# A hybrid attention and experts layer on one core: decay columns, level steps, start and end rearranged

## The chip, the core and the metric

The kernel runs on one core of a Trainium2 chip. Its metric is the device time of one execution in microseconds, median of several runs. The engines are named as the profile names them: PE (TensorE; PEld are its weight loads), DVE (VectorE), ACT (ScalarE), POOL (GpSimd) and SP (SyncE, which here only issues DMAs). Each engine works through its own queue in order, and the queues wait for one another through semaphores.

## The reference, cut to what matters

256 tokens of width 2048 in float32 go through one layer. An RMS norm and one wide projection give the inputs of two attention-like mixers and of two gates. Mixer A (gated delta rule, 8 heads) needs, per chunk of tokens, the inverse of a unit lower triangular matrix that holds the decayed products of the keys. The mixers are projected, gated, merged, projected again and added to x. Then 32 experts, of which each token takes two, and a final RMS norm.

```python
h = _rmsnorm(x, norm_mix); z = h @ w_in
a_strict = where(strict, einsum("bhnid,bhnjd->bhnij", kb, k) * decay, 0.0)
t_mat = triangular_solve(eye + a_strict, eye, lower=True)
...
x = x + (sigmoid(mix_a) * ya + sigmoid(mix_b) * yb) @ w_out
x = x + _hier_moe(_rmsnorm(x, norm_ffn), ...)
return _rmsnorm(x, norm_final)
```

## The kernel before, in words

All work is written out by hand, queue by queue; nothing is planned by a compiler.

*Projection.* The weights come in chunks of 1 MB (four rows of 512 columns per partition) through a ring of four slots. A chunk is split in two parts that add up to the float32 value: ACT rounds it (`high`, line 671), DVE subtracts (`low`, line 942), and PE takes three products for each pair of operands (lines 1377 to 1379). So a chunk is 24 matmuls of 512 columns. ACT may be three chunks ahead of PE (NSPLIT). Four chunks make a block of 512 output columns, which ACT evacuates (lines 686 and 689). The token side is split likewise: PE transposes x (line 1400), ACT makes hT_hi (line 708), DVE makes hT_lo (line 956), in eight steps of two pieces.

*Order of the steps.* PE's attention steps (STEPS) are spread between the chunks: SPANS says how many chunks follow each step, and `fill` puts them there. Steps write two PSUM bank pairs in turn, so that a step waits until the one before the last is drained (`open_pair`). ACT and DVE follow the same order through `Splitter`: ahead of a result they split the chunks that PE will have used by then, except for the last, which `rest` makes up.

*Mixer A, per group g of four heads (eight units of 128 by 128).* PE transposes q, k and v (zqT, zkT, zvT, line 1540). POOL writes the decay of each token as 128 equal columns, gB (line 568), and PE multiplies gB with an upper triangle (gcb, line 1543), which gives the running sum of the decay in every row. DVE and ACT make the two decay matrices Dm and DT from it; DVE makes the convolution (line 1120), paced by the chunks behind gcb; ACT squares q and k (line 808), which ssq (line 1549) sums. Then ktok, vtok, khT, A (line 1559), PT (line 1560). DVE multiplies A with Dm (line 1139). The inverse is built in seven levels. For each, POOL masks Dm (line 605) into one of two buffers. Y1 (line 1562) is the first; each further level is Y (line 1567), a copy of it by ACT (line 813), dU (line 1570), dT (line 1573), two subtractions by DVE (lines 1154 and 1157) and one chunk of projection. Behind dU64 come wT (line 1589) and the rest of the step.

*Experts.* 16 pairs of experts. SP reads w1, w3 and w2, 24 pieces of 1 MB for a pair, into 16 slots. PE frees a slot when it has used it (`slotM_free`), and SP waits for that. PE multiplies with w1 and w3 (line 1753), transposes the hidden part, multiplies with w2 (line 1773: four steps t, each over all 2048 columns), and after ACT's copies (line 910) combines the result with the tokens' weights (line 1789), which DVE adds to x1 (line 1340). At the end ACT squares x1 (line 921), DVE sums (line 1350), POOL takes the root (lines 661 and 662), and DVE multiplies each row of 2048 by root and norm (line 1354), which SP stores (line 476).

## Time and profile before

| | us |
|---|---|
| median of 3 runs | 1897.27 |
| lowest, highest | 1896.11, 1897.51 |
| the profiled execution's own time | 1895.62 |
| its span | 1893.8 |

| engine | busy us | share |
|---|---|---|
| PE | 1785.6 | 94% |
| PE weight load | 1111.2 | 59% |
| DVE | 637.7 | 34% |
| ACT | 432.1 | 23% |
| POOL | 181.1 | 10% |

The granted clock of PE has a mean of 0.983 of full speed over the span. 537 MB are moved, at a mean of 284 GB/s. The shares are means over stages with different limits, so they don't tell what a change in one stage is worth. A line of the timeline has start, duration, engine, line of the kernel, operation, result and operands with their sizes, how many instructions are merged, and in brackets how long the engine had been idle before and what released it. Ends of matmuls are modelled. A float32 matmul stands as two records, so eight units of a step are 16 records, and eight transposes are 8.

### The profile page before, as it was taken

What the parts mean: (1) busy time and instruction counts of PE and PEld (TensorE: products, weight loads), DVE (VectorE), ACT (ScalarE), POOL (GpSimd) and SP (SyncE); (2) the same over time, 40 slices, a digit from 0 to 9 for tenths busy, and PEclk for the clock granted to TensorE, in tenths of its full rate; (3) what the DMA queues carried; (4) which work ended last, traced back from release to release, by engine and by line L of the source; (5) the groups of instructions that cost most, each with busy time, mean ns of one, the idle gap of its engine ahead of it and who ended that gap; (6) DMA issues with size and microseconds to landing.
All of it is one profiled execution on the core that took longest, in us unless ns stands there. A gap on an engine that the chain in (4) does not pass through costs nothing.

```text
span 1893.8 us, 21446 instructions
## 1 busy us (share of the span) xinstructions
PE 1785.6 (94%) x8774; PEld 1111.2 (59%) x8774; DVE 637.7 (34%) x670; ACT 432.1 (23%) x449; POOL 181.1 (10%) x235
## 2 busy tenths in 40 slices
PE   5999999989898899999899999999999999999996
PEld 4778877878787778888744344434344343443432
DVE  3256776533573355554302121112112021110112
ACT  4254354422442243334300000000000000000001
POOL 4000040430133010000000000000000000000000
PEclk8999999999999999999899999999999999999998
DMA  6445444422352245565999999999999999999996
GB/s 186 133 162 172 154 135 134 156 89 90 113 176 67 89 124 194 178 222 178 377 384 412 420 421 421 422 422 422 422 422 422 422 422 421 422 422 422 421 421 260
DMA packets 120460, 537.43 MB, mean 284 GB/s; under 512 B 8700, under 2 KB 8764, under 8 KB 70348
## 3 DMA queue, kind: packets, MB, share of 16 engines
q1 hardware_dynamic: 119808, 535.86, 72.5%
q0 software_dynamic: 592, 0.69, 0.3%
q8 instruction: 47, 0.77, 0.2%
q14 instruction: 13, 0.11, 0.0%
HBM read 534.42 MB, written 2.10 MB: 283 GB/s over the span
## 4 chain that ended last, share of the span: by engine, by line
PE 79%; DMA 15%; DVE 2%; ACT 2%; POOL 1%; issue 1%; DVEq 0%; SPq 0%; POOLq 0%; ACTq 0%
PE psum L1753 19%; DMA arena<-in_w 14%; PE psum L1377 12%; PE psum L1378 12%; PE psum L1379 12%; PE psum L1773 6%; PE psum L1789 6%; PE psum L1716 5%; PE psum L1570 1%; PE psum L1567 1%; PE psum L1573 1%; DMA arena<-in_w_in 1%; PE psum L1410 1%; PE psum L1469 1%; POOL arena L568 1%
## 5 line engine op out<-in xcount | busy, mean ns | idle before, releaser
L1753 PE MATMUL psum<-arena 128*64 128x512 f32 x2048 | 445.9, 594 | 13.3 <-DMA arena<-in_w 12.8
L942 DVE TENSOR_TENSOR w_lo<-arena,w_hi 128x2048 fp32r<-128x2048 f32 x120 | 276.1, 2303 | 326.7 <-ACT w_hi L671 320.3
L1377 PE MATMUL psum<-w_hi,hT_hi 128*128 128x512 f32 x832 | 336.6, 405 | 13.5 <-DVE hT_lo L956 12.2
L1378 PE MATMUL psum<-w_lo,hT_hi 128*128 128x512 f32 x832 | 332.0, 399 | 0.0
L1379 PE MATMUL psum<-w_hi,hT_lo 128*128 128x512 f32 x832 | 331.9, 399 | 0.0
L1753 PEld LDWEIGHTS psum<-arena 128*64 128x64 f32 x2048 | 143.9, 137 | 310.6 <-issue 282.2
L671 ACT ACTIVATE w_hi<-arena 128x2048 fp32r<-128x2048 f32 x120 | 229.4, 1915 | 292.0 <-PE psum L1379 286.3
L1773 PE MATMUL psum<-arena 128*64 128x512 f32 x1024 | 227.4, 598 | 13.0 <-DMA arena<-in_w 12.1
L1377 PEld LDWEIGHTS psum<-w_hi,hT_hi 128*128 128x128 f32 x832 | 158.7, 191 | 51.2 <-DVE hT_lo L956 12.3
L1379 PEld LDWEIGHTS psum<-w_hi,hT_lo 128*128 128x128 f32 x832 | 158.0, 190 | 38.6
L1378 PEld LDWEIGHTS psum<-w_lo,hT_hi 128*128 128x128 f32 x832 | 158.4, 190 | 36.4
L1773 PEld LDWEIGHTS psum<-arena 128*64 128x64 f32 x1024 | 71.3, 137 | 157.1 <-issue 128.1
L1324 DVE TENSOR_TENSOR arena<-psum,arena 128x512 f32<-128x512 f32 x64 | 44.2, 691 | 315.7 <-PE psum L1716 315.7
L1716 PEld LDWEIGHTS psum<-arena 128*128 128x128 f32 x1024 | 119.8, 194 | 26.1 <-issue 26.0
L1716 PE MATMUL psum<-arena 128*128 128x128 f32 x1024 | 127.3, 281 | 0.0
L1789 PE MATMUL psum<-arena 128*128 128x512 f32 x256 | 112.6, 593 | 0.0
L1340 DVE TENSOR_TENSOR arena<-arena,psum 128x512 f32<-128x512 f32 x128 | 87.9, 687 | 42.0 <-PE psum L1789 42.0
L900 ACT ACTIVATE arena<-psum 128x512 f32<-128x512 f32 x16 | 9.6, 597 | 358.9 <-PE psum L1753 358.9
L910 ACT ACTIVATE arena<-psum 128x512 f32<-128x512 f32 x64 | 38.2, 597 | 227.3 <-PE psum L1773 227.3
L641 POOL TENSOR_TENSOR arena<-arena 128x128 f32<-128x128 f32 x30 | 11.4, 399 | 783.4 <-PE psum L1716 751.0
L1331 DVE SCALAR_TENSOR_TENSOR arena<-arena,psum 128x512 f32<-128x512 f32 x16 | 11.0, 687 | 215.1 <-ACT arena L900 215.1
L1334 DVE TENSOR_TENSOR arena<-arena,psum 128x512 f32<-128x512 f32 x16 | 11.0, 687 | 214.2 <-PE psum L1753 214.2
(328 smaller groups left out, 1250.3 us busy)
## 6 DMA issues: line engine op xcount, KB each, us to landing
arena<-in_w SPq DMA_DIRECT2D x384, 1024.0 KB, 25.9
arena<-in_w_in SPq DMA_DIRECT2D x88, 1024.0 KB, 5.0
arena<-in_w_out SPq DMA_DIRECT2D x16, 1024.0 KB, 5.1
arena<-in_w_oa SPq DMA_DIRECT2D x8, 1024.0 KB, 5.0
arena<-in_w_ob SPq DMA_DIRECT2D x8, 1024.0 KB, 5.0
arena<-in_x SPq DMA_DIRECT2D x4, 1024.0 KB, 7.6
out_y<-arena SPq DMA_DIRECT2D x2, 1024.0 KB, 4.1
arena<-in_norm_final SPq DMA_DIRECT2D x1, 1024.0 KB, 18.6
```

What stands on the lines that cost most here:

```text
L671: nc.scalar.activation(w_hi[x % NSPLIT], ringA[:, x % RING_A, :], ACT.Copy).then_inc(sem("w_hi"), 1)
L910: nc.scalar.activation(Ysb[:, k * CB:(k + 1) * CB], bank(4 + k), ACT.Copy).then_inc(sem("yev"), 1)
L942: tt(w_lo[x % RING_A], ringA[:, x % RING_A, :], w_hi[x % NSPLIT].bitcast(F32), ALU.subtract)\
L1324: tt(xeT[u][:, 4 * b:4 * b + 4, :], bank(2 + b % 2).rearrange("p (k s) -> p k s", k=4), nffn[:, 4 * b:4 * b + 4].unsqueeze(2).to_broadcast ...
L1340: tt(x1[:, m, k * CB:(k + 1) * CB], x1[:, m, k * CB:(k + 1) * CB], bank(4 + (2 * k + m) % 4), ALU.add).then_inc(sem("xadd"), 1)
L1377: mm(m_banks[m], lhs[0][:, k0 + k, ms], wh[:, cs], start=(start and k == 0), stop=False)
L1378: mm(m_banks[m], lhs[0][:, k0 + k, ms], wl[:, cs], start=False, stop=False)
L1379: i = mm(m_banks[m], lhs[1][:, k0 + k, ms], wh[:, cs], start=False, stop=(stop and k == CT - 1))
L1716: i = mm(bank(2 + b % 2)[:, k * P:(k + 1) * P], h2[:, m, 4 * b + k, :], sel[:, m * P:(m + 1) * P], start=(m == 0), stop=(m == NM - 1))
L1753: i = mm(bank(w)[e * CAP:(e + 1) * CAP, :], xeT[u][:, CT * q + k, e * CAP:(e + 1) * CAP], src[e][:, k * CB:(k + 1) * CB], start=(q == 0 an ...
L1773: i = mm(bank(4 + k)[e * CAP:(e + 1) * CAP, :], aT[:, t * P + e * CAP:t * P + (e + 1) * CAP], src[e][:, k * CB:(k + 1) * CB], start=(t == ...
L1789: mm(bank(4 + j % 4), comb[u][:, m * P:(m + 1) * P], Ysb[:, k * CB:(k + 1) * CB], start=True, stop=True).then_inc(sem("cmb"), 1)
```

## The change

It touches five places.

1. *Start.* PE transposes the first half of x's tokens before it waits for the second half. ACT and DVE make three of the eight token steps ahead of chunk 0's split, two behind it, then split chunks 1 and 2, then make the last three; ACT's squares for the first norm come last. PE waits for hT_lo piece by piece. POOL builds its masks and the iota before it issues the DMAs of the twelve small tensors.
2. *Decay columns.* gB isn't written any more: the stationary operand of gcb is the decay column itself, read with a step of zero.
3. *First level.* POOL masks Dm for level 1 (mask[1]) right when Dm is scaled by beta, into gB; DVE multiplies A into gB first and into Dm second. POOL's mask loop begins at level 2. Each Y is copied in two halves, each as soon as PE has it, and dU waits for each half by itself.
4. *Chunks.* In group 1 gcb is followed by eight chunks instead of nine, dU64 by one instead of none.
5. *End.* The last pair's w2 is read in pieces of half the columns and two steps t (rows of 4 KB instead of 8), so that the first 1024 columns are complete after two of four pieces. Copies, combines and squares follow by quarters. The first 1024 columns are multiplied by the final norm ahead of the root, on POOL and DVE, and scaled by the root on ACT, the others are done on DVE as before; the output is stored in four halves. POOL takes one root for each half of the tokens, with 1/D and eps taken into the squares and the sum.

Some semaphores are merged, and SP's loop over the pairs ends one step earlier, with the last two pairs written out. The diff, cut to its core:

```diff
-     {"gcb": 9, "ssq": 1, "vtok": 1, "khT": 1, "PT": 0, "dT2": 1, "dT4": 1, "dT8": 1, "dT16": 1, "dT32": 1,
-      "wT": 1, "o": 2}.items()},
+     {"gcb": 8, "ssq": 1, "vtok": 1, "khT": 1, "PT": 0, "dT2": 1, "dT4": 1, "dT8": 1, "dT16": 1, "dT32": 1,
+      "dU64": 1, "wT": 1, "o": 2}.items()},
...
+            more_rounds = sp.value_load(rounds_i[0:1, 1:2], min_val=0, max_val=SEQ // CAP - 1)
+            end = more_rounds * (PAIRS // UNROLL) + (PAIRS // UNROLL - 1)
+            with sp.Fori(1, end) as i:
...
+            load_pair(PAIRS - 2, more_rounds * PAIRS + (PAIRS - 2), 0, 0, PER_PAIR)
+            load_pair(PAIRS - 1, more_rounds * PAIRS + (PAIRS - 2), 1, 0, 2 * RING_M - PER_PAIR + 8)
+            for j in range(16, PER_PAIR):
+                piece, e = divmod(j - 16, 2)
+                slot = (PER_PAIR + j) % RING_M
+                sp.wait_ge(sem("slotM_free"), more_rounds * (PAIRS * PER_PAIR) + ((PAIRS - 1) * PER_PAIR + j + 1))
+                sp.dma_start(ringM[slot].rearrange("p (t n) -> p t n", t=2),
+                             w2_h[2 * (PAIRS - 1) + e, :, 2 * (piece % 2):2 * (piece % 2) + 2,
+                                  (piece // 2) * HALF:(piece // 2 + 1) * HALF]).then_inc(sem(f"slotM{slot // 2}"), 16)
...
             for m in range(NM):
-                wait(sp, ("y_ready", m + 1))
-                sp.dma_start(y_v[:, m, :], x1[:, m, :]).then_inc(sem("y_out"), 16)
-            sp.wait_ge(sem("y_out"), 16 * NM)
+                for h, name in enumerate(("y_lo", "y_hi")):
+                    wait(sp, (name, m + 1))
+                    sp.dma_start(y_v[:, m, h * HALF:(h + 1) * HALF], x1[:, m, h * HALF:(h + 1) * HALF])\
+                        .then_inc(sem("y_out"), 16)
+            sp.wait_ge(sem("y_out"), 32 * NM)
...
+                           allow_small_or_imprecise_dtypes=True).then_inc(sem("pool_setup"), 1)
+            def small(dst, src, name):
+                pool.dma_start(dst, src, allow_slow_non_contiguous=True).then_inc(sem(name), 16)
...
-                for h in range(GH):
-                    for n in range(NM):
-                        u = h * NM + n
-                        i = nc.gpsimd.tensor_scalar(T_["gB"][:, u * P:(u + 1) * P], ones,
-                                                    mh(gdec)[:, n, g * GH + h:g * GH + h + 1], None, ALU.mult)
-                i.then_inc(sem("gB"), 1)
-
                 wait(pool, ("expD", g + 1))
...
                 bv = mh(beta)[:, :, g * GH:(g + 1) * GH].rearrange("p n h -> p h n").unsqueeze(3)\
                     .to_broadcast([P, GH, NM, P])
                 nc.gpsimd.tensor_tensor(T_["Dm"].rearrange("p (h n t) -> p h n t", h=GH, n=NM),
                                         T_["Dm"].rearrange("p (h n t) -> p h n t", h=GH, n=NM), bv,
                                         ALU.mult).then_inc(sem("DA"), 1)
+                pool.wait_ge(sem("DA"), g + 1)
+                nc.gpsimd.tensor_tensor(units(T_["gB"]), units(T_["Dm"]),
+                                        mask[1].unsqueeze(1).to_broadcast([P, GU, P]), ALU.mult)\
+                    .then_inc(sem("D1"), 1)
...
-                wait(pool, full(f"gcb.{g}"))
-                for i, b in enumerate(LEVELS):
+                for i, b in list(enumerate(LEVELS))[1:]:
...
-            wait(pool, ("ss4", 1))
-            link(nc.gpsimd.tensor_scalar(ss2, ss2, 1.0 / D, EPS, ALU.mult, ALU.add))
-            nc.gpsimd.tensor_tensor(rstd2, ss2, pw[:, 0:NM], ALU.pow).then_inc(sem("rstd3"), 1)
+            more_rounds = pool.value_load(rounds_i[0:1, 1:2], min_val=0, max_val=SEQ // CAP - 1)
+            more_rounds = pool.value_load(rounds_i[0:1, 1:2], min_val=0, max_val=SEQ // CAP - 1)
+            pool.wait_ge(sem("nfin_in"), 16)
+            for m in range(NM):
+                pool.wait_ge(sem("xadd"), more_rounds * (8 * PAIRS) + (8 * PAIRS + m + 1))
+                nc.gpsimd.tensor_tensor(xn[:, m, 0:CB], x1[:, m, 0:CB], nfin[:, 0:CB], ALU.mult)\
+                    .then_inc(sem("pool_end"), 1)
+            for m in range(NM):
+                pool.wait_ge(sem("dve_end"), NM + m + 1)
+                nc.gpsimd.tensor_tensor(rstd2[:, m:m + 1], ss2[:, m:m + 1], pw[:, 0:1], ALU.pow)\
+                    .then_inc(sem("pool_end"), 1)
...
+            def high_tokens(i):
                 act.wait_ge(sem("xTp"), i + 1)
                 for k in range(2):
                     j = nc.scalar.activation(hTh[:, 2 * i + k, :], bank(i)[:, k * SEQ:(k + 1) * SEQ], ACT.Copy,
                                              scale=nmix[:, 2 * i + k:2 * i + k + 1])
                 j.then_inc(sem("hTh"), 1)
+            act.wait_ge(sem("nmix_in"), 16)
+            for i in range(3):
+                high_tokens(i)
+            sp_ = Splitter(high, evac)
+            for i in range(3, 5):
+                high_tokens(i)
             sp_.second()
+            for i in range(5, 8):
+                high_tokens(i)
+            for m in range(NM):
+                nc.scalar.activation(Z1[:, m * D:(m + 1) * D], xs0[:, m, :], ACT.Square,
+                                     accum_out=ss1[:, m:m + 1]).then_inc(sem("ss1"), 1)
...
-                    result(f"Y{b}" + s)
-                    nc.scalar.activation(T_["Y"], pair(f"Y{b}" + s), ACT.Copy).then_inc(sem("Y"), 1)
+                    sp_.before(f"Y{b}" + s)
+                    act.wait_ge(sem("Y_half"), g * 6 + i + 1)
+                    nc.scalar.activation(T_["Y"][:, 0:512], pair(f"Y{b}" + s)[:, 0:512], ACT.Copy)\
+                        .then_inc(sem("Y"), 1)
+                    wait(act, full(f"Y{b}" + s))
+                    nc.scalar.activation(T_["Y"][:, 512:1024], pair(f"Y{b}" + s)[:, 512:1024], ACT.Copy)\
+                        .then_inc(sem("Y"), 1)
...
+            def squares(k, m):
+                act.wait_ge(sem("xadd"), last * 8 + (8 + 2 * k + m + 1))
+                nc.scalar.activation(junk[:, (2 * k + m) * CB:(2 * k + m + 1) * CB], x1[:, m, k * CB:(k + 1) * CB],
+                                     ACT.Square, scale=float(D) ** -0.5,
+                                     accum_out=ssq4[:, m, k:k + 1]).then_inc(sem("ss3"), 1)
+            def evict(k):
+                if k % 2 == 0:
+                    act.wait_ge(sem("down"), last * (NC - 1) + k // 2 + 1)
+                else:
+                    act.wait_ge(sem("slotM_free"), last * PER_PAIR + (RING_M + 16 + 4 * (k // 2 + 1)))
+                nc.scalar.activation(Ysb[:, k * CB:(k + 1) * CB], bank(4 + k), ACT.Copy).then_inc(sem("yev"), 1)
...
+                    squares(k, m)
+            act.wait_ge(sem("pool_end"), NM)
+            act.wait_ge(sem("dve_end"), NM)
+            for m in range(NM):
+                act.wait_ge(sem("pool_end"), NM + m + 1)
+                nc.scalar.activation(x1[:, m, 0:HALF], xn[:, m], ACT.Copy, scale=rstd2[:, m:m + 1])\
+                    .then_inc(sem("y_lo"), 1)
...
+                dve.wait_ge(sem("D1"), g + 1)
+                tt(T_["gB"], pair("A" + s), T_["gB"], ALU.mult).then_inc(sem("L_first"), 1)
...
+                dve.wait_ge(sem("L_first"), g + 1)
...
+                    if k == 2 and not more:
+                        dve.wait_ge(sem("nfin_in"), 16)
+                        for m in range(NM):
+                            dve.wait_ge(sem("xadd"), n * 8 + (8 + NM + m + 1))
+                            tt(xn[:, m, CB:HALF], x1[:, m, CB:HALF], nfin[:, CB:HALF], ALU.mult)\
+                                .then_inc(sem("dve_end"), 1)
...
-            dve.wait_ge(sem("ss3"), NM * NC)
-            nc.vector.reduce_sum(ss2, ssp.rearrange("p (m c) -> p m c", m=NM), axis=AX.X).then_inc(sem("ss4"), 1)
-            dve.wait_ge(sem("nfin_in"), 16)
-            wait(dve, ("rstd3", 1))
             for m in range(NM):
-                stt(x1[:, m, :], x1[:, m, :], rstd2[:, m:m + 1], nfin, ALU.mult, ALU.mult).then_inc(sem("y_ready"), 1)
+                dve.wait_ge(sem("ss3"), NM * NC - 1 + m)
+                nc.vector.reduce_sum(ss2[:, m:m + 1], ssq4[:, m], axis=AX.X).then_inc(sem("dve_end"), 1)
+            for m in range(NM):
+                wait(dve, ("pool_end", NM + m + 1))
+                stt(x1[:, m, HALF:D], x1[:, m, HALF:D], rstd2[:, m:m + 1], nfin[:, HALF:D], ALU.mult, ALU.mult)\
+                    .then_inc(sem("y_hi"), 1)
...
-            for i in range(8):
-                for k in range(2):
-                    for m in range(NM):
+                for i in range(8):
+                    for k in range(2):
                         j = tr(bank(i)[:, (k * NM + m) * P:(k * NM + m + 1) * P], xs0[:, m, 2 * i + k::KT], ident)
-                j.then_inc(sem("xTp"), 1)
-            wait(pe, ("hTl", 8))
+                    if m == NM - 1:
+                        j.then_inc(sem("xTp"), 1)
             for x in range(FIRST_BLOCKS * BCH):
+                if x < BCH:
+                    wait(pe, ("hTl", 2 * x + 2))
...
-                wait(pe, ("gB", g + 1))
-                lvl("gcb", lambda o, u, sl: mm(o[:, sl], T_["gB"][:, sl], upT, start=True, stop=True))
+                lvl("gcb", lambda o, u, sl: mm(o[:, sl], mh(gdec)[:, u % NM, g * GH + u // NM:g * GH + u // NM + 1]
+                                               .to_broadcast([P, P]), upT, start=True, stop=True))
...
-                pe.wait_ge(sem("L"), 7 * g + 1)
+                pe.wait_ge(sem("L_first"), g + 1)
                 lvl("Y1", lambda o, u, sl: mm(o[:, sl], T_["gB"][:, sl], ident, start=True, stop=True))
                 for j, b in enumerate(LEVELS[1:]):
                     L = T_["gB"] if (j + 1) % 2 == 0 else T_["L1"]
-                    pe.wait_ge(sem("L"), 7 * g + j + 2)
+                    pe.wait_ge(sem("L"), 6 * g + j + 1)
                     pe.wait_ge(sem("U"), 7 * g + j + 1)
-                    lvl(f"Y{b}", lambda o, u, sl: mm(o[:, sl], L[:, sl], T_["U"][:, sl], start=True, stop=True))
-                    pe.wait_ge(sem("Y"), 6 * g + j + 1)
+                    def level_y(o, u, sl):
+                        i = mm(o[:, sl], L[:, sl], T_["U"][:, sl], start=True, stop=True)
+                        if u == GU // 2 - 1:
+                            i.then_inc(sem("Y_half"), 1)
+                        return i
+                    def level_du(o, u, sl):
+                        if u % (GU // 2) == 0:
+                            pe.wait_ge(sem("Y"), 2 * (6 * g + j) + u // (GU // 2) + 1)
+                        return mm(o[:, sl], T_["T"][:, sl], T_["Y"][:, sl], start=True, stop=True)
+                    lvl(f"Y{b}", level_y)
                     pe.wait_ge(sem("T"), 6 * g + j + 1)
-                    lvl(f"dU{b}", lambda o, u, sl: mm(o[:, sl], T_["T"][:, sl], T_["Y"][:, sl], start=True,
-                                                      stop=True))
+                    lvl(f"dU{b}", level_du)
...
+            def last_down(n, u, arrived):
+                def combine(k):
+                    pe.wait_ge(sem("yev"), n * NC + (k + 1))
+                    for m in range(NM):
+                        j = 2 * k + m
+                        if j >= 4:
+                            pe.wait_ge(sem("xadd"), n * 8 + (j + 5))
+                        mm(bank(j % 4), comb[u][:, m * P:(m + 1) * P], Ysb[:, k * CB:(k + 1) * CB], start=True,
+                           stop=True).then_inc(sem("cmb"), 1)
+                for piece in range(4):
+                    src = arrived(16 + 2 * piece)
+                    half, tp = divmod(piece, 2)
+                    for k in range(2):
+                        for t in range(2):
+                            for e in range(2):
+                                i = mm(bank(4 + 2 * half + k)[e * CAP:(e + 1) * CAP, :],
+                                       aT[:, (2 * tp + t) * P + e * CAP:(2 * tp + t) * P + (e + 1) * CAP],
+                                       src[e][:, t * HALF + k * CB:t * HALF + (k + 1) * CB],
+                                       start=(tp == 0 and t == 0), stop=(tp == 1 and t == 1))
+                        if tp == 1 and k == 0:
+                            i.then_inc(sem("down"), 1)
+                    i.then_inc(sem("slotM_free"), 2)
+                    if piece:
+                        combine(piece - 1)
+                combine(NC - 1)
...
```

## Rows read from the trace of the kernel before

**Rows 1.** busy by stage; columns: window, busy us (instructions) per engine, clock, DMA, GB/s
```profile
256.00:700.00 444.00, 404.55 (x2173) 343.90 (x2172) 231.09 (x210) 164.24 (x148) 114.90 (x78) 0.97 0.36 114
...
1290.00:1871.00 581.00, 554.46 (x2682) 231.06 (x2680) 88.75 (x129) 35.90 (x65) 21.33 (x56) 1.00 1.01 421
1871.00:1893.80 22.80, 10.72 (x32) 4.02 (x32) 10.26 (x11) 8.17 (x20) 0.91 (x2) 0.81 0.24 100
```

**Rows 2.** timeline of the start; columns: start, us, engine, line, operation [idle before, releaser]
```profile
2.43 2.54 POOL L500 DMA_DIRECT2D arena<-in_w_in  x2 [0.30 <-POOL arena L496]
...
10.02 5.98 PE L1400 MATMUL psum<-arena 128*128 128x128 f32 x32 [10.02 <-DMA arena<-in_x]
10.23 0.56 POOL L500 DMA_DIRECT2D arena<-in_b_re  x1
...
11.96 10.60 POOL L532 TENSOR_SCALAR_AFFINE_SELECT arena<-arena 128x128 f32<-128x128 f32 x14
17.60 1.91 ACT L671 ACTIVATE w_hi<-arena 128x2048 fp32r<-128x2048 f32 x1 [5.69 <-DMA arena<-in_w_in]
19.41 5.92 ACT L708 ACTIVATE hT_hi<-psum,arena 128x256 fp32r<-128x256 f32 x16
19.54 2.29 DVE L942 TENSOR_TENSOR w_lo<-arena,w_hi 128x2048 fp32r<-128x2048 f32 x1 [19.54 <-ACT w_hi L671]
21.75 6.35 DVE L956 SCALAR_TENSOR_TENSOR hT_lo<-psum,arena,hT_hi 128x256 fp32r<-128x256 f32 x16
...
28.16 0.80 PE L1377 MATMUL psum<-w_hi,hT_hi 128*128 128x512 f32 x1 [12.16 <-DVE hT_lo L956]
```

**Rows 3.** busy time of all engines in two stretches of the start
```profile
9.00:14.00 5.00, 3.98 (x19) 4.01 (x20) 0.00 (x0) 2.00 (x2) 4.92 (x13) 1.00 1.09 153
...
17.00:23.00 6.00, 0.00 (x0) 0.00 (x0) 3.46 (x5) 5.40 (x12) 5.83 (x9) 0.59 1.04 388
```

**Rows 4.** timeline, groups 0 and 1: the gcb matmuls, and the copy of zkT.1
```profile
287.70 3.68 PE L1543 MATMUL psum<-arena 128*128 128x128 f32 x16 [2.77 <-POOL arena L568]
...
498.20 3.78 PE L1543 MATMUL psum<-arena 128*128 128x128 f32 x16 [3.81 <-POOL arena L568]
...
493.53 1.22 DVE L1099 COPY arena<-psum 128x1024 f32<-128x1024 f32 x1
```

**Rows 5.** line 813, ScalarE's copy of Y: instructions, and who waited for them (us, times)
```profile
L813 ACT ACTIVATE arena<-psum x12: 1023/1023/1023, 386.6 to 653.8; 128x1024 f32<-128x1024 f32 x12
...
  PE psum L1570: 13.4, 12
```

**Rows 6.** GpSimd's masks (line 605) of 570 to 590 us; timeline of group 1's first levels
```profile
L605 POOL TENSOR_TENSOR arena<-arena x2: 2350/3336/4322, 580.7 to 585.0; 128x1024 f32<-128x1024 f32 x2
...
579.41 1.22 DVE L1139 TENSOR_TENSOR arena<-psum,arena 128x1024 f32<-128x1024 f32 x1 [2.25 <-PE psum L1559]
...
585.09 3.50 PE L1562 MATMUL psum<-arena 128*128 128x128 f32 x16 [3.93 <-POOL arena L605]
589.96 2.02 PE L1567 MATMUL psum<-arena 128*128 128x128 f32 x16 [1.36 <-issue]
```

**Rows 7.** timeline of PE behind the last level of group 1
```profile
660.12 2.07 PE L1589 MATMUL psum<-arena 128*128 128x128 f32 x8 [3.20 <-DVE arena L1154]
```

**Rows 8.** timeline of the end of the convolution and of the squares in group 1
```profile
541.87 1.92 ACT L671 ACTIVATE w_hi<-arena 128x2048 fp32r<-128x2048 f32 x1 [3.71 <-PE psum L1379]
...
546.75 2.00 ACT L808 ACTIVATE arena<-arena 128x1024 f32<-128x1024 f32 x2
...
552.86 3.63 PE L1549 MATMUL psum<-arena 128*128 128x1 f32 x32
```

**Rows 9.** chain that ended last (start, us, what); timeline of the two products
```profile
1871.09 3.65 PE psum L1773 x16
1874.74 7.08 PE psum L1789 x16
...
1884.68 4.61 DVE L1354 SCALAR_TENSOR_TENSOR arena<-arena 128x2048 f32<-128x2048 f32 x2 [1.20 <-POOL arena L662]
```

## What the change will do to the time: the prediction

> **What bounds the kernel now.** I read the busy time by stage first [rows 1]. From 256 to 700 us the tensor engine (PE) is busy 404.6 of 444.0 us while DMA uses 0.36 of its time: the attention stage is bound by PE, and what can be won there are its 39 us of gaps. From 1290 to 1871 us, in the experts, DMA is busy throughout (share 1.01, 421 GB/s) and PE is not (554 of 581 us): there the weights set the pace, and the change leaves their bytes alone. Behind the last weights stands a tail of 22.8 us at 100 GB/s. Next I went through the timeline of each place that the diff touches, for the wait that ends last there. The kernel is a chain: start, attention with gaps, weight stream, tail. The experts' weights are read into slots that PE's progress frees, so what is won before them starts the stream earlier by as much; I count such gains in full.
>
> The sum is made against the profiled execution: span 1893.8, its own time 1895.6 us, which is 1.65 us under the median of 1897.27.
>
> **The start.** In [rows 2] the first weight chunk is in at 17.60 us, ScalarE (ACT) rounds it (1.9) and VectorE (DVE) forms the rest (2.3, from 19.54): 21.8. PE starts only at 28.16, because DVE then forms all sixteen hT_lo pieces (6.35) behind ACT's sixteen hT_hi pieces (5.92). With three of the eight groups made ahead of the chunk, PE waits for chunk 0 alone: 28.16 − 21.8 = 6.4 us, if the chunk lands as before.
> It should land earlier, since POOL now issues the small tensors' DMAs behind its masks. In [rows 3] the traffic falls to 153 GB/s from 9 to 14 us with the DMA engines fully busy, and is back at 388 from 17 to 23. x is in at 10.0 [rows 2]. A chunk is 1.05 MB, 2.6 us at 400 GB/s: 12.5. By then the three groups are nearly ready: the transposes of x's first half run before its second half is in, the others take half of 5.98 us, and ACT's six pieces take 6 × 0.37 = 2.2 us from 10.4 on, to 12.7. Rounded at 14.6, rest at 16.9, PE starts at 17.0: gain 11.1 us. Bounds 6.4 (chunk as before) and 11.8.
> What must stay hidden: ACT makes tokens 3 and 4 (1.5), rounds chunks 1 and 2 (to about 22), makes tokens 5 to 7 (2.2) and both squares (as wide as a rounding, 2.1 each), to 28.3, and then waits for the small tensors. POOL's masks, which took from 10.8 to 22.6 [rows 2], now stand ahead of its issues, which took from 2.43 to 10.8: the last is out at 22.9. I let it land by 31, an estimate: 8 us, as long as chunk 0 took from x's landing on. Chunk 3 is then ready at 31 + 1.9 + 2.3 = 35.2, and PE asks for it at 17.0 + 7.3 + 2 × 5.6 = 35.5 (7.3: the first chunk begins at the 1.2 GHz level; 5.6: the period of ACT's rounding in [rows 8]). The cover is thin: each later us costs one.
> The Trainium skill speaks against this move (SBUF — State Buffer, SBUF: two separate sides): the descriptors of a DMA issued from GpSimd are written by that engine, and a VectorE operation in a two-port mode locks it out of the shared ports. VectorE had nothing to do before 19.54 [rows 2] and now works from 10.9 on; no row here shows such a delay. By the rule the result is the second rival.
>
> **Decay columns.** POOL no longer writes gB; PE loads the decay column with a step of zero. In [rows 4] PE waits 2.77 us for POOL at 287.70 and 3.81 at 498.20, and the 16 records then take 3.68 and 3.78 us, where the same shape takes 2.02 at 589.96 [rows 6]: the 1.2 GHz level against 2.4. PE itself was free at 284.9 and 494.4; in group 1 DVE's copy of zkT ends at 494.8 and is now late. Group 0: 284.9 + 2.3 = 287.2 instead of 291.4, 4.2 us. Group 1: 494.8 + 2.1 = 496.9 instead of 502.0, 5.1. Sum 9.3 us. A load with step zero has no row; the nearest, loads of 128 columns, hide beside the matmuls. I take no extra. Bounds 7.5 (0.1 us more for each of 16 units) and 10.3.
>
> **Level copies in halves.** In [rows 5] PE waited 13.4 us for ACT's copy of Y, 12 times 1.11. The copy of the first half can start when four units are done, 1.1 us into Y's 2.0, and takes 0.6 (half of 1.02 and a little): over at 1.75, so that dU starts when Y ends. The second half is copied from 2.0 to 2.6, and dU wants it at 2.9. All but 0.05 of each gap goes: 12.7 us. Each period shrinks from 12.4 to 11.3; ACT's two halves, one rounding and now and then an evacuation fill 4.4 of it. Bounds 10 (where ACT is evacuating at the time) and 13.4.
>
> **First level masked ahead.** In [rows 6] PE waits 3.93 us for POOL's first mask in group 1 and runs Y1 at the lower level, 3.50 us. Now DVE multiplies A with the already masked decay (1.2 us from 579.41), and behind it comes the ordinary product, which also frees the bank: 581.8. Y1 then ends at 583.7. Next late is POOL's mask for level 2, which starts after the second product, beside DVE: [rows 6] have 4.32 us for the mask beside DVE and 2.35 for the one alone. Started at 581.8 it is done at 586.2 at most, and U, which DVE makes behind a low part and PT's product, at 586.4. Y2 starts there instead of at 589.96: 3.5 us. If the new wait of 2.7 us lowers the clock, Y2 costs 1.7 more; I take 2.5. Bounds 0 and 3.5. In group 0 a chunk covers this wait already: 0.
> The Trainium skill explains the two lengths (same page and section: VectorE and GpSimd lock a shared pair of ports for a whole instruction). If the lock never bit, the mask would be done at 584.1 and the sum would be the same, as U is later.
> POOL's added mask (2.4 to 4.3 us) delays rqk; DVE scales ktok up to 3 us later, and khT follows only behind a chunk of 5.6 us: 0, at most 1.
>
> **The moved chunk.** Behind dU64 of group 1 PE waits 3.20 us for DVE and then takes 2.07 us [rows 7] for eight records, half of a level's sixteen, which is again the lower level: 1.0 too much. A chunk there covers both, 4.2. But gcb keeps eight chunks to cover the convolution. PE reaches ssq at 552.86 in [rows 8]; a chunk less is 547.3, while ACT's squares end at 546.75 + 2.00 = 548.75. Exposed 1.3, net 2.9 us. Bounds 1 and 4.2.
>
> **The tail.** Before [rows 9]: last weights at 1871.09, matmuls 3.65, eight combines 7.08, then add, square, sum, power and two products to 1889.3, and 4.5 for the store. After: pieces of 2.1 MB come 4.98 us apart (421 GB/s), and PE needs 3.65 + 1.77 (a quarter of 7.08) for each, so it begins the last 0.9 late. With 3.65 and two combines' pairs (3.5) the last combine ends 8.0 after the last weights, before 10.7: 2.7 us. Behind it, before, 12.0 us. Now add, square, sum and power, 2.0 for the first row of tokens and 0.8 more for the second, and two products of half the width on each of two engines (2 × 1.2): the last store goes out at 4.3 and carries 0.5 MB, 3.7: 8.0, a gain of 4.0. The final norm's MB is last in the queue, 2.5 us behind the weights, and the columns multiplied ahead fit before the last combines. The last 8 MB have rows of 4 KB instead of 8; the nearest rates are 388 for the chunks' 2 KB rows [rows 3] and 421, a loss of 0 to 1.7 us; I take 0.5. Tail 6.2 us. Bounds 3 and 8.
>
> Merged semaphores and the restated loop on SP's queue move no wait: 0.
>
> **Sum.** 11.1 + 9.3 + 12.7 + 2.5 + 2.9 + 6.2 = 44.7 us: 1897.3 − 44.7 = 1852.6 us.
>
> **Rivals.**
> *Copies stay visible* (0.10). If the wait inside dU, or an ACT that is busy when half of Y is done, brings back what the halves win, 12.7 us stay: 1865.3. For it: ACT also evacuates blocks there. Against: in [rows 5] all 12 gaps are the bare copy, so ACT was never late.
> *The small tensors come late* (0.14). If they land at 36 us instead of 31, or chunk 0 lands as before, some 4.7 us of the start's gain go: 1857.3. For it: the thin cover.
> *Step zero is slow* (0.03), the one that ends slower than before: if the array reads a column of step zero slowly, 16 units pay. From 44.7 / 16 = 2.8 us each the whole gain is gone; at 4 us the change costs 64 − 44.7 = 19.3 us: 1916.6. Against: loads in [rows 4] show no price beside the matmuls.
> *The stream is not moved* (0.02): if the weights' stream kept its time, only the tail would count, 1891 to 1897. Against: its slots are freed by PE alone.
>
> **Numbers.** The forecast has 0.71. The range goes from 1844 (all upper bounds together are 51 us, 1846, and 2 for scatter) to 1868 (visible copies, and 2.7 of other lower bounds). 0.2%, 3.8 us, is about what a measurement of this kernel can tell from no change: faster 0.95, within it 0.02, slower 0.03.
>
> **What would show it.** First projection matmul at 17 us; gcb without a wait, at 2.1 to 2.3 us; none of PE's waits at dU; one wait of 2 to 3 us ahead of Y2 in group 1; 1.3 us ahead of ssq in group 1 and none behind dU64; the span's end 16 us behind the last weights. It is wrong if PE waits for w_lo of chunk 3, or if the experts begin less than 35 us earlier.

## The result, and the profile after

The changed kernel takes 1856.2 us where the kernel before, on the same chip, takes 1897.4: a ratio of 0.9779, 95% interval 0.9762 to 0.9796 (four executions of each; those of the changed kernel lie between 1852.4 and 1856.8). A second set, taken later beside the last experiments, gave 1856.5 against 1896.9, 0.9788 (0.9774 to 0.9801). The forecast was 1852.6 with a range of 1844 to 1868, and "faster". The profiled execution of the changed kernel takes 1856.06 us with a span of 1854.2; before it was 1895.62 and 1893.8. So the traces differ by 39.6 us, and the sum of the prediction was 44.7.

The same three stages as in [rows 1], by the busy time in windows (window, busy us and instructions of PE, PEld, DVE, ACT and POOL, clock, DMA share, GB/s):

```profile
243.00:664.00 421.00, 404.46 (x2187) 344.87 (x2186) 232.96 (x212) 168.78 (x161) 101.31 (x62) 0.98 0.39 123
1254.00:1834.00 580.00, 555.01 (x2682) 231.59 (x2680) 90.09 (x131) 38.63 (x71) 21.32 (x56) 1.00 1.01 421
1834.00:1854.15 20.15, 10.43 (x36) 3.32 (x30) 9.14 (x12) 7.62 (x16) 5.54 (x4) 0.86 0.32 127
```

PE's work in the attention stage is the same 404.5 us, but it now takes 421 us and not 444: the gaps went. The experts run at the same 421 GB/s, only earlier.

The start, answering [rows 2] (start, us, engine, line, operation, idle before and its releaser):

```profile
9.56 1.28 ACT L716 ACT_TABLE_LOAD   x1 [9.56 <-PE psum L1474]
10.86 2.31 ACT L716 ACTIVATE hT_hi<-psum,arena 128x256 fp32r<-128x256 f32 x6
13.02 1.94 ACT L685 ACTIVATE w_hi<-arena 128x2048 fp32r<-128x2048 f32 x1
...
17.43 0.76 PE L1452 MATMUL psum<-w_hi,hT_hi 128*128 128x512 f32 x1 [6.37 <-DVE w_lo L998]
...
20.02 0.56 POOL L541 DMA_DIRECT2D arena<-in_b_re  x1
```

PE multiplies from 17.43 instead of 28.16. The chunk is in before ACT asks for it at 13.02 (no idle time ahead of w_hi). A load of ACT's table, 1.28 us, now stands between the transposed tokens and the first high half.

The decay columns and group 1, answering [rows 4], [rows 6], [rows 7] and [rows 8]; TensorE's timeline and GpSimd's mask:

```profile
274.99 1.98 PE L1618 MATMUL psum<-arena 128*128 128x128 f32 x16
474.77 2.05 PE L1618 MATMUL psum<-arena 128*128 128x128 f32 x16 [0.41 <-DVE arena L1162]
523.28 6.12 PE L1625 MATMUL psum<-arena 128*128 128x1 f32 x32 [1.50 <-ACT arena L828]
...
555.65 2.02 PE L1638 MATMUL psum<-arena 128*128 128x128 f32 x16 [0.75 <-DVE arena L1204]
560.07 2.02 PE L1645 MATMUL psum<-arena 128*128 128x128 f32 x16 [2.40 <-DVE arena L1212]
...
625.49 1.05 PE L1675 MATMUL psum<-arena 128*128 128x128 f32 x8
...
555.59 4.33 POOL L611 TENSOR_TENSOR arena<-arena 128x1024 f32<-128x1024 f32 x1 [11.00 <-DVE arena L1204]
```

The gcb products (L1618) have no wait for GpSimd and take 2 us instead of 3.7. Y1 (L1638) waits 0.75 and Y2 (L1645) 2.40, for VectorE's U and not for the mask beside it, which is over at 559.92, only 0.05 us before U (558.75 + 1.22 = 559.97). wT (L1675) has no wait. Ahead of ssq (L1625) there is one of 1.50 us, and ssq itself takes 6.12 us where it took 3.63 [rows 8]: that was in no part of the prediction.

The levels, answering [rows 5]: ACT's copy of a half (line 834) and who waited for it.

```profile
L834 ACT ACTIVATE arena<-psum x12: 597/599/599, 372.9 to 617.3; 128x512 f32<-128x512 f32 x12
...
  PE psum L1653: 0.5, 3
```

13.4 us in 12 waits have become 0.5 in 3 (0.15 us each).

The tail, answering [rows 9]; timelines of TensorE, VectorE, GpSimd and the stores on SP's queue:

```profile
1821.02 8.78 PE L1834 MATMUL psum<-arena 128*64 128x512 f32 x32 [0.88 <-ACT arena L927]
...
1837.15 3.65 PE L1834 MATMUL psum<-arena 128*64 128x512 f32 x16
1840.73 3.70 PE L1825 MATMUL psum<-arena 128*128 128x512 f32 x8
...
1845.33 0.58 POOL L675 TENSOR_TENSOR arena<-arena 128x1 f32<-128x1 f32 x1 [3.98 <-DVE arena L1425]
1846.02 1.28 DVE L1428 SCALAR_TENSOR_TENSOR arena<-arena 128x1024 f32<-128x1024 f32 x1
1846.19 1.53 POOL L675 TENSOR_TENSOR arena<-arena 128x1 f32<-128x1 f32 x1 [0.28 <-DVE arena L1425]
...
1847.20 2.94 SPq L493 DMA_DIRECT2D out_y<-arena  x4
```

The traffic behind the stores' issue (window, busy us of the five engines, clock, DMA share, GB/s):

```profile
1848.00:1853.00 5.00, 0.00 (x0) 0.00 (x0) 1.04 (x1) 0.91 (x1) 0.00 (x0) 0.56 1.00 400
```

The four pieces (L1834) no longer wait for a DMA, where the last one did in [rows 9]: PE is late, not the weights. Its first two pieces take 8.78 us and the last 3.65.

**Where the 39.6 us came from.** Take the same matmul in both traces and subtract its start: the lead of the changed kernel. It is 10.7 us at the first projection matmul, 10.1 at zkT of group 0 (the low clock level lasted 1.3 us longer at the earlier start, and the first chunk took 7.96 us instead of 7.35), 14.4 behind gcb, 12.8 at A, 20.0 behind the levels of group 0, 25.2 behind gcb of group 1, 26.3 at A, 29.9 at Y2, 36.9 at the last dU, 34.6 at wT, 36.2 at u0, 36.3 when w3 is through, and 39.6 at the end. Twice it falls or stands still where the change does nothing good: between gcb and A of group 0 (−1.6) and of group 1 (+1.1, though a chunk of 5.6 us less stands there).

### The profile page after: what moved, and what is told of

It reads as the page before. It is cut to its first block, busy times and chain, and to the rows that moved or that the text cites. A ratio compares the mean times of both kernels' runs of the same rounds, so it can differ in the third digit from the quotient of the medians.

```text
span 1854.2 us, 21397 instructions
## 1 busy us (share of the span) xinstructions
PE 1782.7 (96%) x8774; PEld 1109.0 (60%) x8774; DVE 640.2 (35%) x676; ACT 436.2 (24%) x463; POOL 170.2 (9%) x221
## 4 chain that ended last, share of the span: by engine, by line
PE 81%; DMA 13%; DVE 2%; ACT 2%; SPq 1%; issue 1%; POOL 0%; POOLq 0%; DVEq 0%; ACTq 0%
PE psum L1868 18%; DMA arena<-in_w 13%; PE psum L1452 12%; PE psum L1453 12%; PE psum L1454 12%; PE psum L1890 7%; PE psum L1905 5%; PE psum L1802 5%; PE psum L1653 1%; PE psum L1659 1%; PE psum L1645 1%; PE psum L1834 1%; SPq L459 1%; DVE w_lo L998 1%; PE psum L1486 1%
## 5 line engine op out<-in xcount | busy, mean ns | idle before, releaser
L1868 PE MATMUL psum<-arena 128*64 128x512 f32 x2048 | 446.1, 594 | 13.3 <-DMA arena<-in_w 12.8
L1868 PEld LDWEIGHTS psum<-arena 128*64 128x64 f32 x2048 | 143.9, 137 | 310.7 <-issue 282.3
L1890 PE MATMUL psum<-arena 128*64 128x512 f32 x960 | 211.3, 595 | 10.5 <-DMA arena<-in_w 10.5
L1890 PEld LDWEIGHTS psum<-arena 128*64 128x64 f32 x960 | 66.0, 137 | 144.5 <-issue 118.9
L1905 PE MATMUL psum<-arena 128*128 128x512 f32 x240 | 105.5, 592 | 0.0
```

The costliest lines, as they stand in the source:

```text
L1868: i = mm(bank(w)[e * CAP:(e + 1) * CAP, :], xeT[u][:, CT * q + k, e * CAP:(e + 1) * CAP], src[e][:, k * CB:(k + 1) * CB], start=(q == 0 an ...
L1890: i = mm(bank(4 + k)[e * CAP:(e + 1) * CAP, :], aT[:, t * P + e * CAP:t * P + (e + 1) * CAP], src[e][:, k * CB:(k + 1) * CB], start=(t == ...
L1905: mm(bank(4 + j % 4), comb[u][:, m * P:(m + 1) * P], Ysb[:, k * CB:(k + 1) * CB], start=True, stop=True).then_inc(sem("cmb"), 1)
```

## The experiments

All edits are to the changed kernel. Each row gives the median, the ratio to the kernel before on the same chip in the same set, and the difference to the changed kernel. That difference goes by the time saved against before: 41.2 us for the first eight rows, 40.4 for the last four, which had the changed kernel beside them.

| kernel | us | ratio (95%) | against the changed one |
|---|---|---|---|
| small_first | 1861.0 | 0.9807 (0.9790 to 0.9825) | +5.3 |
| decay_pool | 1865.0 | 0.9834 (0.9816 to 0.9851) | +9.2 |
| whole_copy | 1872.3 | 0.9870 (0.9853 to 0.9888) | +16.6 |
| late_mask | 1858.8 | 0.9804 (0.9787 to 0.9822) | +3.0 |
| chunk_back | 1859.6 | 0.9795 (0.9779 to 0.9812) | +3.1 |
| chunk_from_khT | 1855.6 | 0.9773 (0.9757 to 0.9790) | −0.9 |
| wide_ssq | 1853.5 | 0.9771 (0.9755 to 0.9787) | −3.0 |
| tail_warm | 1856.6 | 0.9775 (0.9758 to 0.9793) | +0.1 |
| after_again | 1856.5 | 0.9788 (0.9774 to 0.9801) | 0 |
| chunk_ahead | 1853.0 | 0.9763 (0.9749 to 0.9776) | −3.5 |
| wide_ahead | 1849.2 | 0.9748 (0.9735 to 0.9761) | −7.3 |
| combined | 1845.7 | 0.9735 (0.9721 to 0.9748) | −10.8 |

The intervals of the ratios are 3.2 to 3.4 us wide to either side, 2.5 in the last four rows, and the executions of one kernel can lie 7 us apart (1851.35 to 1858.40 in tail_warm). So differences of 3 us (late_mask, chunk_back, wide_ssq, and chunk_ahead's 3.5) are not shown by the times alone; for those the traces are read.

**1. The start (small_first).** The block of twelve small loads goes back ahead of the masks:

```
+            def small(dst, src, name):
+                pool.dma_start(dst, src, allow_slow_non_contiguous=True).then_inc(sem(name), 16)
...
             def masks(upper):
...
-            def small(dst, src, name):
-                pool.dma_start(dst, src, allow_slow_non_contiguous=True).then_inc(sem(name), 16)
```

> Only one part of the changed kernel is undone: GpSimd issues the twelve small loads ahead of the masks again, as before. My theory: ahead of the token and weight loads they take the transfer queues' time at the start (the weights' first chunk came at 17.6 us before), so the first projection matmul moves from 17.4 us back to 21.5 to 22.5, ScalarE's table load and order being as in the changed kernel; the whole kernel is 4 to 5 us slower than the changed one (1860 to 1861.5). The rest of the 10.7 us gained at the start (some 6) is then the order of ScalarE's squares. Rival: the order of the small loads is of no account and all 10.7 came from the order on ScalarE: the first projection matmul stays at 17.4 and the time at 1856.

5.3 us slower. The start of its timeline:

```profile
18.56 1.91 ACT L685 ACTIVATE w_hi<-arena 128x2048 fp32r<-128x2048 f32 x1 [3.58 <-DMA arena<-in_w_in]
...
22.94 0.76 PE L1452 MATMUL psum<-w_hi,hT_hi 128*128 128x512 f32 x1 [8.66 <-DVE w_lo L998]
```

ACT waits for the chunk until 18.56 and PE starts at 22.94, 5.5 us later. So of the 10.7 us at the start, 5.5 are the order of the loads; the 5.2 that are left go, by subtraction, to the order of ACT's and VectorE's pieces, which no run undoes. The first half of the theory holds (4 to 5 us were expected); the rival is out.

**2. The decay columns (decay_pool).** GpSimd's sixteen instructions for gB are back, and in TensorE's queue:

```
-                lvl("gcb", lambda o, u, sl: mm(o[:, sl], mh(gdec)[:, u % NM, g * GH + u // NM:g * GH + u // NM + 1]
-                                               .to_broadcast([P, P]), upT, start=True, stop=True))
+                wait(pe, ("gB", g + 1))
+                lvl("gcb", lambda o, u, sl: mm(o[:, sl], T_["gB"][:, sl], upT, start=True, stop=True))
```

> Only one part is undone: GpSimd writes the broadcast decay columns (16 instructions of it, 8 per group) and gcb's matmuls take them from there, with the wait for it. My theory: gcb costs again what it cost before, 4.3 us more in group 0 and 5.1 in group 1; 1865 to 1866. Rival: since the step-zero operand and the older buffer differ in the weight load as well, part of the gain was in the matmuls themselves, and with the wait satisfied early (the start being earlier, GpSimd may be ahead) gcb takes 2.0 to 2.5 us without a wait: within 1 us of 1856.

```profile
277.23 3.56 PE L1630 MATMUL psum<-arena 128*128 128x128 f32 x16 [2.38 <-POOL arena L584]
...
480.33 3.78 PE L1630 MATMUL psum<-arena 128*128 128x128 f32 x16 [3.83 <-POOL arena L584]
```

9.2 us slower, with the waits of [rows 4] back although the kernel runs 10 us ahead: GpSimd starts when gdec or oaT are there, not when it likes. The theory's 9.4 holds.

**3. The copies (whole_copy).**

```
-                    nc.scalar.activation(T_["Y"][:, 0:512], pair(f"Y{b}" + s)[:, 0:512], ACT.Copy)\
-                        .then_inc(sem("Y"), 1)
...
+                    nc.scalar.activation(T_["Y"], pair(f"Y{b}" + s), ACT.Copy).then_inc(sem("Y"), 1)
```

> Only one part is undone: ScalarE copies each level's Y in one instruction of 1024 columns and TensorE waits for all of it. My theory: each of the 12 levels gives back 1.2 us (a copy of 1.02 in place of a last half of 0.6 that is begun while TensorE works, and the dU step's start), 14.4 us in all: 1870 to 1871. Rival: half of the levels' gain came from elsewhere (the clock being kept up through shorter gaps), so less comes back: 1862 to 1866.

16.6 us slower, a little over the theory's 14.4. Two levels of group 0:

```profile
385.07 1.95 PE L1640 MATMUL psum<-arena 128*128 128x128 f32 x16
388.22 2.02 PE L1645 MATMUL psum<-arena 128*128 128x128 f32 x16 [1.21 <-ACT arena L833]
...
397.48 1.95 PE L1640 MATMUL psum<-arena 128*128 128x128 f32 x16
```

A level takes 12.41 us from Y to Y (L1640), and 11.10 in the changed kernel (382.90 to 394.00 there). That is 1.31 for each of 12 levels: the wait of 1.21 and 0.1 behind it.

**4. The first level (late_mask).** The product D1 ahead of A and VectorE's extra product go; GpSimd's loop masks all seven levels behind A:

```
-                for i, b in list(enumerate(LEVELS))[1:]:
+                for i, b in enumerate(LEVELS):
```

> Only one part is undone: the first level's mask is made by GpSimd behind A again, and not ahead of it, with VectorE's extra product gone. My theory: in each group TensorE waits again for GpSimd's mask ahead of Y1: the stretch from A to Y2 takes 3.5 us longer in group 1 and at least 2 in group 0; 1860 to 1864. Rival: the level itself took no time from the mask, and the 3.6 us in group 1 came from the clock staying up; then the wait for the mask is under 1 us and the time within 1.5 of 1856.

3.0 us slower, less than the theory's 1860 to 1864, and the traced loss is in group 1 alone:

```profile
327.59 3.63 PE L1618 MATMUL psum<-arena 128*128 128x1 f32 x32
...
552.57 3.79 PE L1631 MATMUL psum<-arena 128*128 128x128 f32 x16 [3.93 <-POOL arena L607]
557.72 3.75 PE L1638 MATMUL psum<-arena 128*128 128x128 f32 x16 [1.36 <-issue]
```

In group 0, A to Y2 takes 12.50 us here (356.25 to 368.75) and in the changed kernel alike (359.23 to 371.73); the "at least 2 in group 0" of my expectation was wrong, and the prediction's zero right. In group 1 the wait of 3.93 [rows 6] is back. The trace shows something else too: up to ssq of group 0 (L1618 here) TensorE's instructions are those of the changed kernel, and yet ssq took 3.63 us and not 4.77, and from its start to A there are 28.7 us and not 31.8. No edit accounts for these 3.1 us, nor for the 3.2 at the same place of group 1 (24.7 and 27.9), and with them the profiled execution, 1855.57, is no slower than that of the changed kernel.

**5. The moved chunk (chunk_back, chunk_from_khT).** In the table of group 1:

```
-     {"gcb": 8, "ssq": 1, "vtok": 1, "khT": 1, "PT": 0, "dT2": 1, "dT4": 1, "dT8": 1, "dT16": 1, "dT32": 1,
-      "dU64": 1, "wT": 1, "o": 2}.items()},
+     {"gcb": 9, "ssq": 1, "vtok": 1, "khT": 1, "PT": 0, "dT2": 1, "dT4": 1, "dT8": 1, "dT16": 1, "dT32": 1,
+      "dU64": 0, "wT": 1, "o": 2}.items()},
```

This is chunk_back; chunk_from_khT has 9 for gcb, 0 for khT and 1 for dU64.

> Only the moved chunk is undone (nine chunks behind gcb of group 1, none behind its last level's dU). My prediction said that the move is worth 2.9 us, so this would be 2.9 slower: 1859. My theory now, from the trace of the changed kernel: it is worth nothing, since the wait of 1.50 us ahead of ssq and the longer stretch at the low clock level behind it (ssq 6.12 us, where before it took 3.63) eat the 4.2 to 4.7 us behind dU: within 1 us of 1856, ssq of group 1 without a wait and 3.6 us long, and the wait ahead of wT back at 3.2 us. Rival: the long stretch at the low level has nothing to do with the chunk, and ssq of group 1 stays at 5 us or more here as well; then this is 3 us slower than the changed kernel or more.

3.1 us slower by the medians: my theory, formed from the trace of the changed kernel, isn't borne out, and the prediction's 2.9 is near what was measured. What I had missed:

```profile
626.22 1.30 PE L1675 MATMUL psum<-arena 128*128 128x128 f32 x8 [4.03 <-DVE arena L1220]
634.38 1.05 PE L1676 MATMUL psum<-arena 128*128 128x128 f32 x8
```

With the halved copies TensorE reaches the end of the levels sooner, so the wait ahead of wT is 4.03 us and not 3.20 [rows 7], and the chunk behind it takes 8.16 us from L1675 to L1676 where it takes 6.51 in the changed kernel. The moved chunk thus saves 4.03 + 1.65 = 5.7 us behind dU64 and costs the wait of 1.5 and the clock ahead of A: from gcb to oaT of group 1 the two traces differ by 2.1 us. So 2.1 us are shown, and the rest of the 3.1 is within the scatter.

> The chunk behind the last dU of group 1 stays, but it is taken from behind khT of that group and not from behind gcb (which has nine again). Theory: ssq has no wait and behind khT only ScalarE's copy of 1.1 us is laid open, so this is 0.4 us faster by the waits and up to 3 more by the clock: 1852.5 to 1855.5. Rival: the gap behind khT lets the clock fall at A, PT and Y1 instead, and the time is that of the changed kernel, 1855.5 to 1858.

0.9 us faster, which the intervals can't tell from nothing; the time is the rival's, not the theory's. ssq has no wait, but the 1.11 us behind khT are laid open as expected, and then Y1 waits:

```profile
547.88 2.05 PE L1635 MATMUL psum<-arena 128*128 128x128 f32 x16 [1.11 <-ACT arena L830]
554.37 2.66 PE L1638 MATMUL psum<-arena 128*128 128x128 f32 x16 [2.65 <-DVE arena L1204]
```

A starts 3.3 us sooner than in the changed kernel. 1.9 of them are given back at Y1, which waits for VectorE's second product with A, the one that frees the bank (2.65 us and not 0.75). Behind that wait the clock falls, as the rival said, though one step later than it said: Y1 takes 2.66 us and Y2 3.76, and the granted clock is 0.55 from 557 to 563 us. At wT nothing is left (625.53 and 625.49).

**6. The clock behind ssq (wide_ssq, then chunk_ahead and wide_ahead).** The granted clock around ssq of the two groups, for the kernel before, the changed one and late_mask (windows; the clock is the third number from the right):

Before, group 1:

```profile
552.00:558.00 6.00, 6.00 (x43) 5.54 (x42) 1.56 (x2) 1.91 (x1) 4.82 (x2) 0.95 0.51 175
558.00:564.00 6.00, 6.00 (x23) 4.74 (x23) 2.29 (x1) 0.17 (x1) 1.72 (x1) 0.76 0.00 0
```

Changed kernel, groups 0 and 1:

```profile
327.00:333.00 6.00, 6.00 (x37) 5.76 (x36) 1.12 (x2) 1.91 (x1) 5.99 (x3) 0.72 0.54 178
...
523.00:529.00 6.00, 5.72 (x31) 5.75 (x32) 0.86 (x1) 3.10 (x4) 5.92 (x3) 0.60 0.50 174
529.00:535.00 6.00, 6.00 (x17) 4.79 (x18) 1.91 (x2) 0.00 (x0) 4.23 (x2) 0.55 0.00 0
```

late_mask, group 0:

```profile
327.00:333.00 6.00, 6.00 (x44) 5.54 (x43) 1.29 (x2) 1.91 (x1) 4.83 (x2) 1.00 0.55 178
```

Ahead of ssq the clock is at 1.00 (2.4 GHz) everywhere; behind it TensorE runs at 0.50 (1.2 GHz) for a while, though it is busy throughout: in the changed kernel for most of 12 us in group 1. The suspects are the sixteen products of one column in ssq (32 records) and the wait ahead of it. First the width:

```
-                        i = mm(o[:, 8 * j + u:8 * j + u + 1], T_[f"zT{j}"][:, u * P:(u + 1) * P], ones[:, 0:1],
+                        i = mm(o[:, 64 * (8 * j + u):64 * (8 * j + u + 1)], T_[f"zT{j}"][:, u * P:(u + 1) * P],
+                               ones[:, 0:64], start=True, stop=True)
```

> One size is changed: the matmuls of ssq have 64 moving columns (64 ones in place of one; VectorE reads the first of each 64), with everything else as in the changed kernel. Theory: the granted clock falls behind ssq in every kernel so far because these 16 products of one column give TensorE next to nothing to do; with 64 columns the clock stays at 2.4 GHz through ssq and behind it: ssq takes 3.5 to 4 us, the chunks behind it no longer than others, and both groups together win 4 to 6 us: 1850 to 1852.5. Rival one: the wait of 1.50 us ahead of ssq in group 1 makes the clock fall, not the narrow products: then group 0 wins some 3 and group 1 nothing (1853 to 1854), or neither. Rival two: the level is of another cause (power or chance) and falls here as well: 1855.5 to 1858.

3.0 us faster, as rival one has it: group 0 wins, group 1 doesn't.

```profile
327.00:333.00 6.00, 6.00 (x44) 5.50 (x43) 1.45 (x2) 1.91 (x1) 6.00 (x3) 1.00 0.57 178
...
520.00:526.00 6.00, 5.60 (x30) 5.63 (x31) 0.98 (x1) 3.20 (x4) 5.92 (x3) 0.61 0.55 177
```

So in group 1, with the wait of 1.49 us ahead of ssq, the clock falls with the wide products as well (one traced place). Then the wait, with narrow and with wide products: the chunk behind ssq goes ahead of it, in the same table of group 1:

```
-     {"gcb": 8, "ssq": 1, "vtok": 1, "khT": 1, "PT": 0, "dT2": 1, "dT4": 1, "dT8": 1, "dT16": 1, "dT32": 1,
+     {"gcb": 9, "ssq": 0, "vtok": 1, "khT": 1, "PT": 0, "dT2": 1, "dT4": 1, "dT8": 1, "dT16": 1, "dT32": 1,
```

> In group 1 the one chunk that stood behind ssq is put ahead of it (nine behind gcb, none behind ssq), the chunk behind the last dU stays; no other edit. Theory: the wait of 1.50 us ahead of ssq goes, nothing new shows behind vtok, since its chunk covers the norms, and without the wait the low stretch behind ssq is the short one (4 us in place of 10): 1.5 + 3 us less than the changed kernel, 1851.5 to 1853. Rival one: the low stretch is as long without the wait, as in group 0 of the changed kernel: 1.5 less, 1854.5. Rival two: VectorE's product ahead of khT now shows, TensorE waits for it by 1 us or more ahead of khT, and nothing is won: 1855.5 to 1857.

> The same order in group 1 with the 64-column matmuls of ssq. Theory: with neither a wait ahead of ssq nor narrow products the clock stays at 2.4 GHz in both groups, ssq takes 3.7 us in each, and against the kernel with 64 columns alone (1853.5) the wait of 1.5 and some 3 us of the clock go: 1848.5 to 1850, with a scatter of less than 2 us. Rival: the clock falls behind ssq in group 1 also without the wait: 1852 or more.

chunk_ahead is 3.5 us faster, wide_ahead 7.3; both medians are in the theory's range. wide_ahead, groups 0 and 1:

```profile
328.00:334.00 6.00, 6.00 (x44) 5.55 (x43) 0.68 (x2) 1.91 (x1) 6.00 (x3) 1.00 0.54 178
...
524.00:530.00 6.00, 6.00 (x53) 5.87 (x52) 1.31 (x2) 1.91 (x1) 6.00 (x3) 1.00 0.53 175
```

The clock stays at 1.00 in both, ssq takes 3.68 us in both, and the five executions lie within 2.1 us (less than 2 were expected). The moved chunk leaves a wait of 0.40 us ahead of khT. In chunk_ahead, with one column and no wait, the low stretch of group 1 was short (granted clock 0.85 and 0.86 over 12 us) and that of group 0 stayed; one of its five executions came at 1847.0, the other four within 0.9 us around 1853. With one column the clock fell in group 0 without a wait, with 64 columns it fell in group 1 behind the wait, and only without both did it hold in both groups.

What the clock costs here can be read over all the traces, from the start of ssq to A. In group 0, where TensorE's instructions between the two differ in nothing but the width, the stretch took 28.7, 30.2 or 31.8 us, with a granted clock of 1.00, 0.86 or 0.72 over the first 12 us. With 64 columns it was 28.7 in three of three traces. With one column it was 28.7 once (late_mask), 30.2 in three (the kernel before, decay_pool, tail_warm) and 31.8 in seven. tail_warm and the changed kernel are the same program up to there, so part of this is chance. In group 1, with the same chunks between ssq and A, it took 24.6 us in the two traces without a wait ahead of ssq (the kernel before, chunk_back), and with the wait 27.9 in six, but 26.3 in decay_pool and 24.7 in late_mask: the wait goes with the longer low stretch in most traces and not in all.

That both stretches at 2.4 GHz make the fast executions of the changed kernel (1852.4) is likely, but no trace of such an execution shows it.

**7. The changed kernel again (after_again).**

> The changed kernel itself, unaltered, beside the three that follow: 1856 as the median, and a scatter of 4 us between its executions (1852.4 to 1856.8 so far). If the scatter comes from the clock behind ssq, as I hold, an execution with both ssq steps at 2.4 GHz lies near 1850 and one with both at 1.2 GHz near 1857.

1856.5 as the median, 1854.4 to 1858.3; its profiled execution (1856.5) has ssq at 4.54 and 5.82 us, as the first. Neither of the extremes that I expected for pure cases was profiled.

**8. The tail (tail_warm), and all together (combined).** tail_warm puts two matmuls of 512 columns into each of TensorE's last two waits ahead of the last weights:

```
+                if not more:
+                    for _ in range(2):
+                        mm(bank(2), ident, comb[u][:, 0:2 * P].unsqueeze(1).to_broadcast([P, 2, 2 * P]), start=True, stop=True)
                 pe.wait_ge(sem("hid"), n + 1)
```

The same three lines stand once more behind the transposes of the hidden values, ahead of the wait for aT.

> Four matmuls of 512 columns that nobody reads are put into TensorE's two waits between the last pair's first projections and its last weights (the rest is the changed kernel). Theory: the tail gained 3.4 us in place of 6.2 for one part because the clock stood at 1.2 GHz for most of the first 4 MB of last weights (granted clock 0.66 from 1821 to 1826), so that TensorE was 1.6 us behind the last load when it came to it. With the clock up, TensorE waits for the last piece, and the end comes 1 to 1.7 us earlier: 1854.5 to 1855.2 as the median. Rival: the pace of the combines sets the tail (each piece of 3.65 us and its combines of 1.98), and the time doesn't move; or the added work itself delays the pieces by up to 1 us: 1856 to 1857.

No difference in the time, as the rival said; the 1854.5 to 1855.2 of the theory was missed. The trace has both halves of the reason:

```profile
1820.93 1.98 PE L1877 MATMUL psum<-arena 128*128 128x512 f32 x4
...
1823.22 1.88 PE L1884 MATMUL psum<-arena 128*128 128x512 f32 x4
1825.03 7.09 PE L1834 MATMUL psum<-arena 128*64 128x512 f32 x32
```

The clock is up (1.00 from 1821 to 1826, for 0.66). The first two pieces take 7.09 us and not 8.78, and from the first piece to the last combines there are 18.02 us (to 1843.05) and not 19.71 (to 1840.73). But the added matmuls (1.98 and 1.88 us) are longer than the waits they fill, 0.79 and 0.88, and cost the 1.7 again. combined takes one of 256 columns in each place, together with wide_ahead's edits and a table load made early:

```
+            act.wait_ge(sem("ident"), 1)
+            nc.scalar.activation(ssp[:, 0:1], pw[:, 0:1], ACT.Copy)
             act.wait_ge(sem("nmix_in"), 16)
```

> The kernel before this one with two more edits. A copy of one element on ScalarE at the start, behind GpSimd's identity, makes it load its table while the tokens still come: the first high halves start at 9.6 us and not at 10.9, and the first projection matmul at 16.2 to 16.5 and not at 17.4, unless the first chunk's arrival sets it, in which case it stays at 17.4 (rival). And one matmul of 256 columns in each of TensorE's two waits ahead of the last weights (half a microsecond each, inside waits of 0.79 and 0.88): the clock stays at 2.4 GHz for the first piece and the end is 1.6 us earlier; rival: two short matmuls aren't enough to keep it, and the tail stays. Together 2 to 2.8 us below the kernel with the 64-column matmuls and the chunk ahead: about 1847.

10.8 us under the changed kernel and 3.5 under wide_ahead, where 2 to 2.8 were expected. The traces differ by 4.8: 1.1 us at A of group 1, 2.6 behind Y2, 3.9 at the last products with w3, and 4.8 at the end. No edit accounts for the 1.5 at Y2: the same wait of 2.40 us stands there in both, and the clock fell behind it in wide_ahead and not in combined. Between Y2 and w3 another 1.2 us have no named cause.

```profile
9.88 2.30 ACT L716 ACTIVATE hT_hi<-psum,arena 128x256 fp32r<-128x256 f32 x6 [7.56 <-PE psum L1477]
16.44 0.76 PE L1455 MATMUL psum<-w_hi,hT_hi 128*128 128x512 f32 x1 [5.09 <-DVE w_lo L1000]
...
1811.31 3.65 PE L1837 MATMUL psum<-arena 128*64 128x512 f32 x16 [0.45 <-ACT arena L929]
1815.46 3.65 PE L1837 MATMUL psum<-arena 128*64 128x512 f32 x16 [0.49 <-DMA arena<-in_w]
```

The tokens' high halves start at 9.88 without a table load and PE at 16.44. The first piece takes 3.65 us, and the second waits for its DMA, so at that point the weights set the pace again; the third and fourth don't wait. From the last products with w3 to the end there are 38.3 us here and 39.2 in wide_ahead and in the changed kernel, so the tail's part is about 1 us and not the 1.6 that was expected.

## Why the prediction was right, and where it was off

The forecast case held, with the mechanism of each of its six terms; the total was 5.1 us too high by the traces (39.6 for 44.7). Two terms came out larger than forecast by 2.6 us together and hid as much of what was missing at the tail and at ssq. Part of that was luck of the single trace, as is said at the first level. Point by point, with the measured part as the step of the lead, and what undoing it cost:

| step | predicted | by the lead | undone |
|---|---|---|---|
| start | 11.1 | 10.1 | 5.3 (loads' order alone) |
| decay columns | 9.3 | 9.4 | 9.2 |
| level copies | 12.7 | 14.2 | 16.6 |
| first level | 2.5 | 3.6 | 3.0 |
| moved chunk | 2.9 | 0.4 | 3.1 |
| clock behind ssq, group 0 | none | −1.6 | |
| tail | 6.2 | 3.3 | |

*The start.* The path was as told: the chunk early, three groups ahead of it, PE at 17.43 for 17.0. The 0.4 is less than the table load, 1.28 us, which the prediction didn't see: before, the load ran at 0.81 us, ahead of a square that waited for x until 5.84, and nobody waited for it. Another 0.6 went because the low clock level lasted longer in the first chunk. The small loads, which were the thin cover, were no trouble. The last was issued at 20.02 and landed 6.1 us later, and ACT, which waits for all of them, went on at 26.10 without idle time; 31 was the estimate. Chunk 3 was ready at 30.3, and TensorE came to it at 36.6.

The Trainium skill's rule that spoke against this move (SBUF — State Buffer, SBUF: two separate sides) concerns VectorE's operations in a two-port mode, and no run here shows whether VectorE was in one; so the rule wasn't put to the test. What the traces show is that with VectorE busy from 11.8 us on these loads landed 6.0 to 8.6 us after their issue, and 7.0 to 8.2 before, when it was idle for all of them.

*The decay columns.* Both terms were right to 0.1 us, and a stationary operand of step zero costs nothing that shows: 1.98 and 2.05 us for the products, as for any other operand. That rival is out. (The lower bound, 9.3 less 1.6, is 7.7 and not 7.5.)

*The copies.* The mechanism holds (waits of 0.5 us in all, where none was forecast); the term was short by 1.5, since the gap was counted and not the 0.1 us with which the stalled pipeline starts again.

*The first level.* U was late and not the mask, as told, though by 0.05 us only; Y2 waited 2.40 of the 2.7. The clock did not fall at that wait in this trace, and so the upper bound of 3.5 was the value. That was luck: the same wait of 2.40 us stands in eleven of the traces, and in six of them Y2 ran partly at the lower level (2.55 to 3.54 us, in decay_pool, whole_copy, chunk_back, tail_warm, chunk_ahead and wide_ahead), in five it took 2.02. tail_warm is the changed kernel's program up to there. So the allowance of 1 us for the clock, about half of the full price, was a fair one. Y2 in wide_ahead:

```profile
551.50 3.01 PE L1646 MATMUL psum<-arena 128*128 128x128 f32 x16 [2.40 <-DVE arena L1213]
```

*The moved chunk.* The term was right as an edit by itself (3.1 measured, 2.9 told), but its two halves were both larger. Behind dU64 it covers 4.03 and 1.65 us, not 4.2; ahead of ssq it lays open 1.50 us, for 1.3 told (its own numbers, 548.75 less 547.3, give 1.45), and a longer stretch at 1.2 GHz behind that, which the prediction didn't have. By the lead the step is nearly nothing, because the larger wait ahead of wT exists only with the halved copies and was never in the trace before.

*The clock behind ssq.* This is the step that failed: the sum took the clock ahead of A as given. [rows 8] hold the sign (ssq has 32 records of one column), and the busy time in windows of the trace before, read at 552 to 564 us, has 0.95 and 0.76. A low stretch was there before as well, only shorter. From ssq to A there are 1.6 us more than before in group 0 and 3.3 in group 1 (27.9 for 24.6); the latter is where the moved chunk's gain went, 0.4 by the lead for 2.9. In group 0 nothing was changed between the two, and tail_warm has the 30.2 us of before, so that the 1.6 us there are not shown to be the change's.

The Trainium skill (TensorE: Matmul & The Clock Gate, What's actually happening) says that the number of matmuls a kernel runs before its clock rises differs from run to run of the same kernel. The trace agrees in kind, for the fall: in tail_warm and the changed kernel, the same program up to there, ssq of group 0 took 3.63 and 4.77 us and the stretch to A 30.2 and 31.8.

*The tail.* Two terms were mis-sized. PE was to begin the last piece 0.9 us behind its weights; with the first piece partly at 1.2 GHz (1.7 us longer for two pieces than in tail_warm) it began some 1.9 behind, and the last combines ended about 9.1 us behind the weights and not 8.0 (the weights' end is an estimate, 1835.3: 1871.09 of [rows 9] less the lead of 36.3, plus 0.5). combined, where the clock holds, waits for weights again ahead of the second piece. And behind the last combine (1844.43) the end comes 9.8 us later and not 8.0, and 18.9 behind the weights and not 16. The prediction counted the last store alone, 3.7 us from 4.3 on. But the first store goes out at 1847.20 and the last at 1849.3 (4.9 behind the combine), and then the four share the DMA engines: from 1848 to 1853 these are busy throughout (share 1.00, 400 GB/s), and 2.1 MB at that rate are 5.2 us. The last store landed 4.4 us after its issue, the others after 2.7 us and more. The two stores of before show the same rate, 400 GB/s from 1888 to 1893.

GpSimd's second power takes 1.53 us instead of 0.58 beside VectorE's product, and VectorE waits 0.46 us for it. With the DMA share at 1.00 from 1848 on, it left no gap in the stores' traffic. The Trainium skill explains the long power (SBUF — State Buffer, SBUF: two separate sides): the two engines lock a shared pair of ports for whole instructions. The trace agrees: 1846.19 + 1.53 = 1847.72 is 0.4 us behind the end of the product that VectorE began at 1846.02 (1.28 us), and the second power took 1.53 or 1.54 us in all thirteen traces that have it.

## What to carry to other kernels

Cost a gap of TensorE together with the clock that it may leave behind: a wait of 1.5 us ahead of small products, and products of one column themselves, were in most traces paid again behind them, and mending both was worth 7.3 us here. The clock differs between executions of one program, so look at the same place in several traces before a difference of 1.6 or 3.2 us is put down to an edit. Undo parts one at a time before trusting a difference of two traces: the moved chunk looked worthless by the lead and was worth 3 us as an edit, since another part had enlarged the wait that it covers. Short filler pays only where it is shorter than the wait it fills, and when a path is shortened at its start, look for one-time work, such as a table load, that the old order hid.

## What the runs showed of the hardware beyond what was expected

- The granted clock fell to 1.2 GHz behind products of one column although TensorE was busy by the profile, at 21 of the 22 places with such products that were profiled (two in each of eleven executions, the kernel before among them; the exception is late_mask, group 0); ssq of 64 columns takes as long as ssq of one (3.68 and 3.63 us) and kept 2.4 GHz at all five places where no wait stood ahead of it (group 0 of wide_ssq, both groups of wide_ahead and combined). At the one place with a wait of 1.49 us ahead (wide_ssq, group 1) the clock fell.
- The same wait of 2.40 us ahead of Y2 was followed by a lower clock in six of eleven traces and by none in five.
- A product with a stationary operand of step zero runs like one with an ordinary operand: 1.98 us for 16 records, 2.02 for the same shape [rows 6].
- ACT's table load (1.28 us) can stand on either side of a wait. In the changed kernel, with two waits ahead of the first activation, it ran at 9.56 us, when both were over. With one wait it ran at 0.81 us (before; the activation waited until 5.84) and at 0.82 (combined; until 2.11). What decides this no run shows.
- A store of 512 KB lands 3.6 us after its issue in the middle (2.7 to 4.4 us for the four), one of 1 MB 4.1: by halving it little is won, since the stores share one rate of 400 GB/s. The profile pages' DMA issues, of the changed kernel and of the one before:

```profile
out_y<-arena SPq DMA_DIRECT2D x4, 512.0 KB, 3.6
```

```profile
out_y<-arena SPq DMA_DIRECT2D x2, 1024.0 KB, 4.1
```
